# Sample heads: product order, stores by head, first keys turned under the norm; the first loads in turn; retention's gate and steps moved

## The reference

```
s     = einsum(q, k) * dmask                 # retention, within a chunk
inner = einsum(s, v)
kv    = einsum(k * d_in, v)                  # what the chunk adds to the state
state_new = g_chunk * state + kv             # an output of the program
cross = einsum(q * d_out, state)
on    = (o - mean(o)) / sqrt(var(o) + eps)   # by head, o = inner + cross
mix_r = silu(g) * on * gain                  # concatenated with attention's heads
p = softmax(q . [cache_k, k_new] + window)   # attention of the sample
mix_a = p @ [cache_v, v_new]
```

## Time and profile before

| what | value |
|---|---|
| median of 3 runs | 1917.29 us (1916.12 to 1919.46) |
| profiled execution | 1917.52 us, of which the span of the trace is 1915.7 us |
| busy over the span | PE 89%, PEld 72%, DVE 43%, ACT 29%, POOL 29% |
| granted PE clock, mean | 0.937 |
| bytes moved | 192.19 MB in 137588 packets, 100 GB/s over the span |

### The profile page before, as it was taken

The page is one execution under the profiler, slowest core; times in us unless marked ns, Lnnn a source line. Parts: engine busy times, 40 slices in busy tenths (PEclk is TensorE's granted clock), DMA queues, the critical chain, the costliest instruction groups (busy, mean ns, idle before and its releaser), DMA issues. The chain is left out here.

```text
span 1915.7 us, 22177 instructions
## 1 busy us (share of the span) xinstructions
PE 1698.6 (89%) x8272; PEld 1373.3 (72%) x8272; DVE 832.1 (43%) x1552; ACT 562.3 (29%) x828; POOL 554.9 (29%) x265
## 2 busy tenths in 40 slices
PE   6999999979898688876699689999999999999983
PEld 3778888857676566655588568787878788878862
DVE  4632212046465345566556223333333333333489
ACT  4322222225555155542344221111111111111121
POOL 0233333343000035585000232222222222222354
PEclk9999999979899589986799899999999999999997
DMA  8554433451100667763142211111111111111132
GB/s 290 203 178 155 171 124 121 160 142 56 56 0 24 177 201 219 221 205 111 65 149 80 67 44 44 44 44 44 44 44 44 44 44 44 44 44 44 44 88 93
DMA packets 137588, 192.19 MB, mean 100 GB/s; under 512 B 10034, under 2 KB 86882, under 8 KB 137387
## 3 DMA queue, kind: packets, MB, share of 16 engines
q1 hardware_dynamic: 125396, 168.83, 27.9%
q10 hardware_dynamic: 12128, 22.55, 3.2%
HBM read 162.42 MB, written 28.93 MB: 100 GB/s over the span
## 5 line engine op out<-in xcount | busy, mean ns | idle before, releaser
L2420 POOL TENSOR_TENSOR mlp_w_lo<-w_room,mlp_w_hi 128x2048 fp32r<-128x2048 f32 x31 | 143.7, 4637 | 320.6 <-ACT mlp_w_hi L2416 320.5
L2721 PE MATMUL ps<-mix_hi,mlp_w_hi 128*128 128x512 f32 x512 | 206.4, 403 | 15.1 <-DVE mlp_w_lo L2420 9.6
L2619 DVE TENSOR_TENSOR x<-x,ps 128x512 f32<-128x512 f32 x224 | 154.1, 688 | 141.9 <-PE ps L2792 141.2
L2598 DVE TENSOR_TENSOR mlp_h_lo<-mlp_pos,mlp_h_hi 128x512 fp32r<-128x512 f32 x64 | 69.3, 1083 | 332.8 <-ACT mlp_h_hi L2522 330.7
L2721 PE MATMUL ps<-mix_hi,mlp_w_lo 128*128 128x512 f32 x512 | 203.2, 397 | 0.0
L2721 PE MATMUL ps<-mix_lo,mlp_w_hi 128*128 128x512 f32 x512 | 202.8, 396 | 0.0
L584 POOL TENSOR_TENSOR inp_a_lo<-inp_room,inp_a_hi 128x2048 fp32r<-128x2048 f32 x24 | 111.6, 4649 | 273.8 <-ACT inp_a_hi L718 273.8
L2792 PE MATMUL ps<-mlp_w_hi,mlp_h_hi 128*128 128x512 f32 x448 | 175.8, 392 | 5.5 <-PE ps L2727 5.1
L2792 PE MATMUL ps<-mlp_w_hi,mlp_h_lo 128*128 128x512 f32 x448 | 174.5, 389 | 0.0
L2792 PE MATMUL ps<-mlp_w_lo,mlp_h_hi 128*128 128x512 f32 x448 | 174.3, 389 | 0.0
L637 PE MATMUL ps<-inp_whi,z_hi 128*128 128x512 f32 x384 | 150.3, 391 | 2.4 <-PE ps L637 1.3
(11 more groups left out here) (375 smaller groups left out, 3512.8 us busy)
## 6 DMA issues: line engine op xcount, KB each, us to landing
w_room<-in_w_ff SPq DMA_DIRECT2D x32, 1024.0 KB, 7.0
inp_room<-in_w_ada SPq DMA_DIRECT2D x16, 1024.0 KB
proj<-inp_row ACTq DMA_DIRECT2D x54, 256.0 KB, 2.5
x<-in_cache_k SPq DMA_DIRECT2D x48, 256.0 KB, 5.0
cache_V<-in_cache_v SPq DMA_DIRECT2D x48, 256.0 KB, 4.8
x<-in_x_prompt SPq DMA_DIRECT2D x16, 512.0 KB, 9.5
inp_room<-in_w_ada_f SPq DMA_DIRECT2D x8, 1024.0 KB
x<-in_w_in ACTq DMA_DIRECT2D x16, 512.0 KB, 6.7
```

The lines of the kernel that those rows point to most:

```text
L2420: pool.tensor_tensor(lo, raw, hi.bitcast(F32), ALU.subtract).then_inc(ready, 1)
L2598: dve.tensor_tensor(h_lo[s][:, j, cols], pos[u % 2][:], h_hi[s][:, j, cols].bitcast(F32), ALU.subtract).then_inc(h_ready, 1)
L2619: dve.tensor_tensor(dst, dst, ps[:, 5 + o % 3, :], ALU.add).then_inc(added, 1)
L2721: mm = pe.matmul(ps[:, u, :], w[:, k, j * P:(j + 1) * P], z[:, k, rows], start=(k == 0 and a == 0), stop=(k == KT - 1 and a == 2))
```

## The change

No product, no element-wise operation and no transferred byte of the computation is added or taken away; places, order and waits change.

In the sample heads: the products that are added to the states come before the scores; DVE takes the retention's queries ahead of the attention's, and the gate ahead of the masked scores; the outputs of heads 0, 1 and of heads 2, 3 lie in different banks, so that DVE takes moments and renews states of one pair while PE makes the other; each head's state is stored by itself, and only the next stage waits for these stores; the old states are loaded during the prompt's attention into a part of `x` that it has left; the keys of sequence 0 are loaded before anything is waited for. PE then turns the first three pieces of these keys into banks that are free (`EARLY_ROOMS`), ACT and DVE split them, around the norm; SP loads the first chunk of sequence 1. To make place, the keys lie at `KEYS_AT`, and bias, probabilities and states where the keys were.

In the sample attention: pair 0 starts at its fourth piece; the two tiles for the queries are zeroed by POOL and DVE at once; the bias is waited for where it is used; pair 0's loads of keys and values alternate.

In the retention: POOL waits for both `decayed_keys` before it multiplies the gate; ACT's root is a step of its own; the moments of head 3 come before the gates of heads 2 and 3.

```diff
+KEYS_AT = 3 * S
@@ stage_prompt_attention, SP
+                if pair == 3:
+                    sp.wait_ge(heads_free, 3)
+                    sp.wait_ge(kv_put[0], 64)
+                    smp.load_state(sp, io)
@@ stage_prompt_retention
-        mv = st.sb("mv", [P, TT, 6])
+        moment = [st.sb(f"mv{h}", [P, TT, 6]) for h in range(2)]
...
                 pool.wait_ge(sigmoid_done, a + 1)
+                pool.wait_ge(kd_done, 2)
                 pool.tensor_tensor(g[a][:], g[a][:], eg[a], ALU.mult).then_inc(gate_done, 1)
...
-            for n in range(RH):
-                normalise(n)
-                high_part(n)
+            square_root(0)
+            normalise(0)
+            high_part(0)
+            square_root(1)
+            normalise(1)
+            high_part(1)
+            square_root(2)
+            normalise(2)
+            square_root(3)
+            high_part(2)
+            normalise(3)
+            high_part(3)
...
             moments(2)
+            moments(3)
             gate(2)
-            moments(3)
+            gate(3)
             low_part(2)
-            gate(3)
             low_part(3)
@@ stage_sample_heads, SP
-            for b in range(2):
-                for q in range(4):
-                    sp.dma_start(state[RD * b:RD * (b + 1), q], st_in[b, :, q]).then_inc(s_in, 16)
+            for c in range(3):
+                load_cached(sp, io, "cache_k", K, k_in, 0, c)
             sp.wait_ge(smp.ready, 1)
...
-            for c in range(3):
-                load_cached(sp, io, "cache_k", K, k_in, 0, c)
-            sp.wait_ge(state_done, 1)
-            for b in range(2):
-                for q in range(4):
-                    sp.dma_start(st_out[b, :, q], state[RD * b:RD * (b + 1), q]).then_inc(put, 16)
-            sp.wait_ge(put, 16 * 10)
+            for h in range(RH):
+                sp.wait_ge(state_done, h + 1)
+                for b in range(2):
+                    sp.dma_start(st_out[b, :, :, h], state[RD * b:RD * (b + 1), :, h, :]).then_inc(state_put, 16)
+            sp.wait_ge(keys_turned, 2)
+            load_cached(sp, io, "cache_k", K, k_in, 1, 0)
+            sp.wait_ge(put, 32)
@@ stage_sample_heads, DVE
+            for pair in range(2):
+                heads = (2 * pair, 2 * pair + 1)
+                dve.wait_ge(o_made, pair + 1)
+                for h in heads:
+                    steps.done(dve.bn_stats(stats[:, h, :], o_room(h)))
+                dve.wait_ge(kv_made, 1)
+                for h in heads:
+                    dve.scalar_tensor_tensor(out=state[:, :, h, :], in0=state[:, :, h, :], scalar=GCHUNK_S[h],
+                                             in1=ps[:, 4:8, h * RV:(h + 1) * RV], op0=ALU.mult,
+                                             op1=ALU.add).then_inc(state_done, 1)
...
+            for k in range(EARLY):
+                dve.wait_ge(keys_hi, k + 1)
+                dve.tensor_tensor(keys_part(kT_lo, k), keys_room(k).rearrange("p (c x) -> p c x", c=4),
+                                  keys_part(kT_hi, k).bitcast(F32), ALU.subtract)
@@ stage_sample_heads, PE
+            for k in range(EARLY):
+                pe.wait_ge(k_in[k // 2], CHUNK_IN[k // 2])
+                if k == 1:
+                    pe.wait_ge(state_done, RH)
+                for c in range(4):
+                    for u in range(2):
+                        at = 2 * c + u
+                        mm = pe.transpose(keys_room(k)[:, at * P:(at + 1) * P], K[:, 2 * k + u, c * P:(c + 1) * P], ident[:])
+                mm.then_inc(keys_turned, 1)
@@ stage_sample_attention, SP
-            sp.dma_start(bias, io["bias_s"]).then_inc(tables, 16)
-            for c in range(3):
-                values(0, c)
+            values(0, 0)
+            keys(1, 1)
+            sp.wait_ge(state_put, 16 * 2 * RH)
+            sp.dma_start(bias, io["bias_s"]).then_inc(tables, 16)
+            keys(1, 2)
+            values(0, 1)
+            keys(2, 0)
+            values(0, 2)
+            keys(2, 1)
+            keys(2, 2)
+            values(1, 0)
@@ stage_sample_attention, POOL and DVE
+            pool.memset(q_lo[:].bitcast(F32), 0.0).then_inc(zeroed, 1)
...
-            for x in (q_hi, q_lo):
-                dve.memset(x[:].bitcast(F32), 0.0).then_inc(zeroed, 1)
+            dve.sem_inc(freed, EARLY)
+            dve.memset(q_hi[:].bitcast(F32), 0.0).then_inc(zeroed, 1)
             dve.wait_ge(zeroed, 2)
-            dve.wait_ge(tables, 16)
```

More of the change, by code:

```diff
@@ L1069, in group_norm @@
     e = steps.eng
-    for j in range(n):
-        steps.done(e.bn_stats(stats[rows, j, :], src(j)))
     steps.wait()
@@ L1109, in __init__ @@
             ("dout", [2, P]), ("din", [RH]), ("gch", [2]), ("gain", [RH])))
[L1110 removed]
+        first = 0
         self.v = arena[:, first:first + TT * 2 * RV].rearrange("p (t c) -> p t c", t=TT)
@@ L1487, in load, with load_state @@
             sp.dma_start(dst, io[n]).then_inc(self.tables, 16)
+    def load_state(self, sp, io):
+        src = io["state_ret"][0].rearrange("(q b) h d e -> b d q h e", b=2)
+        for b in range(2):
+            for q in range(4):
+                sp.dma_start(self.state[RD * b:RD * (b + 1), q], src[b, :, q]).then_inc(self.state_in, 16)
     def load_low(self, sp, io):
@@ L1575, in _ @@
             steps = Steps(dve, dve_s)
-            dve.wait_ge(smp.ready, 1)
-            dve.wait_ge(att_turned, 1)
-            for h in range(H):
-                rows = slice(HD * (h % 2), HD * (h % 2 + 1))
-                src = ps[rows, 0, (h // 2) * NS:(h // 2 + 1) * NS].rearrange("p (b t) -> p b t", b=DB)
-                steps.done(dve.tensor_scalar(q_blocks[rows, :, h // 2, h * DS:(h + 1) * DS], src, SCALE, None, ALU.mult))
-            steps.done(dve.tensor_copy(kT_new[:], ps[:, 0, 4 * NS:8 * NS].rearrange("p (c n) -> p c n", n=NS)))
             dve.wait_ge(ret_turned, 1)
@@ L1590, in _ @@
             signal(steps, qT_done)
+            dve.wait_ge(smp.ready, 1)
+            dve.wait_ge(att_turned, 1)
+            for h in range(H):
+                rows = slice(HD * (h % 2), HD * (h % 2 + 1))
+                src = ps[rows, 0, (h // 2) * NS:(h // 2 + 1) * NS].rearrange("p (b t) -> p b t", b=DB)
+                steps.done(dve.tensor_scalar(q_blocks[rows, :, h // 2, h * DS:(h + 1) * DS], src, SCALE, None, ALU.mult))
+            steps.done(dve.tensor_copy(kT_new[:], ps[:, 0, 4 * NS:8 * NS].rearrange("p (c n) -> p c n", n=NS)))
+            signal(steps, att_taken)
+            dve.wait_ge(sigmoid_done, 1)
+            steps.then(dve.tensor_tensor(eg[:], eg[:], x[:, GC:], ALU.mult))
+            steps.then(dve.tensor_tensor(eg[:], eg[:], gain[:], ALU.mult))
             dve.wait_ge(sT_made, 1)
@@ L1630, in _ @@
             mm.then_inc(ret_turned, 1)
-            pe.wait_ge(qT_done, 1)
-            pe.wait_ge(s_in, 128)
             vcols = lambda h: x[:, VC + h * RV:VC + (h + 1) * RV]
-            for h in range(RH):
-                mm = pe.matmul(ps[0:NS, 2, h * NS:(h + 1) * NS], kT[0:RD, h, :], qT[0:RD, h, :], start=True, stop=True)
-            mm.then_inc(sT_made, 1)
             for h in range(RH):
@@ L1640, in _ @@
             mm.then_inc(kv_made, 1)
+            pe.wait_ge(qT_done, 1)
+            for h in range(RH):
+                mm = pe.matmul(ps[0:NS, 2, h * NS:(h + 1) * NS], kT[0:RD, h, :], qT[0:RD, h, :], start=True, stop=True)
+            mm.then_inc(sT_made, 1)
+            pe.wait_ge(s_in, 128)
+            pe.wait_ge(att_taken, 1)
             pe.wait_ge(sT_done, 1)
             for h in range(RH):
-                out = ps[0:NS, 3, h * RV:(h + 1) * RV]
-                pe.matmul(out, sT[:, h * NS:(h + 1) * NS], vcols(h), start=True, stop=False)
+                pe.matmul(o_room(h), sT[:, h * NS:(h + 1) * NS], vcols(h), start=True, stop=False)
                 for b in range(4):
-                    mm = pe.matmul(out, q_masked[:, h, b, :], state[:, b, h, :], start=False, stop=(b == 3))
-            mm.then_inc(o_made, 1)
+                    mm = pe.matmul(o_room(h), q_masked[:, h, b, :], state[:, b, h, :], start=False, stop=(b == 3))
+                if h % 2:
+                    mm.then_inc(o_made, 1)
+            for k in range(EARLY):
+                pe.wait_ge(k_in[k // 2], CHUNK_IN[k // 2])
[6 more added lines that the diff above has]
+                mm.then_inc(keys_turned, 1)
             pe.wait_ge(on_ready, 1)
             for h in range(RH):
-                mm = pe.transpose(ps[:, 2, h * NS:(h + 1) * NS], on[:, h * RV:(h + 1) * RV], ident[0:NS, 0:NS])
+                mm = pe.transpose(ps[:, 0, h * NS:(h + 1) * NS], on[:, h * RV:(h + 1) * RV], ident[0:NS, 0:NS])
             mm.then_inc(o_turned, 1)
@@ L2008, in softmax_top @@
                     dve.wait_ge(turned, AT["P", j - 1, 1] + 1)
+                else:
+                    dve.wait_ge(tables, 16)
                 dve.memset(waited[:], 0.0)
@@ L2055, in _ @@
                 queries(i)
-                keys(i, 0)
-                keys(i, 1)
```

(5 more changed lines are left out.)

112 lines of the change are left out of this document (58 added, 54 removed).

## The result

The changed kernel takes **1892.38 us** (median of 4 runs, 1887.44 to 1895.26), the kernel before 1916.7 us beside it: a ratio of 0.987 (95% interval 0.985 to 0.988), 24 us less. The profiled execution took 1894.17 us, its span 1892.4, at a mean clock of 0.945. The forecast was 1893.4 us.

The account below looks back on a forecast made before the run. PE is near full from 1100 us on, so only its standstills between 617 and 950 us counted. 1917.5 less 11.5 (pair 0, sample heads included) less 12.6 (retention) gave 1893.4 us; range 1886 to 1901 us.

Parts of the forecast that it names:

- Part 1: Sample heads: outputs start 7.5 us earlier, after DVE's masked scores instead of loaded states; the stage gains 7.0 us.
- Part 2: Pair 0 of the sample attention: first scores 2.6 us after the start; ends 11.5 us earlier, sample heads' gain included.
- 6.9 us of products at half speed lose 3.4: Pair 0: clock stays low for 9.5 us after the stage's start, until 659, costing 3.4 us of the lead.
- The lead is carried through: Sample attention from pair 1 on: lists are as before, so the lead gained by pair 0 is kept.
- Part 3: Retention: shorter decayed_keys, then outputs and chunk products at full clock, gain 12.6 us; bounds 7.0 and 13.6.
- Steps at the end: End of retention: head 3's moments before gate 2 gain nothing else and cost 0.1 us; bounds -1 and +1.5.
- A: Sample heads: the clock rises, outputs take half of 9.9 us, 5.0 less; 1888.4 us, chance 0.10.
- B: Retention: PE restarts cold, so only the 7.0 us of decayed_keys is gained; 1899.1 us, chance 0.08.
- C: Retention: the wait moves with POOL to masked_scores(0, 0), leaving a gain of 2.6 us; 1903.4 us, chance 0.05.
- D: Pair 0: loads at 189 GB/s come 4.3 us after PE wants them; 1897.7 us, chance 0.05.
- E: Sample attention: the whole stage loads at 189 GB/s, 33 us more in four pairs; 1926 us, chance 0.02.
- F: Whole kernel: no effect, leads lost before the stages end by an unseen wait; 1917 us, chance 0.03.

Follow-up runs that it names:

- e6: The changed kernel with the old states loaded in the sample heads again, behind the tables; product order kept: 1890.64 us, ratio 0.987.
- e2: The changed kernel without POOL's wait for both decayed_keys in retention, all else kept: 1902.1 us, ratio 0.9922.
- e11: The changed kernel with ACT's sigmoid of the second gate half made twice, lengthening PE's gap in retention: 1894.5 us, ratio 0.9898.
- e9: The changed kernel with pair 0's loads in the old order, sequence 1's first keys no longer loaded in the heads: 1897.17 us, ratio 0.9898.
- e3: The changed kernel with ACT's copies of head pair 1's turned queries and keys ahead of the second gate half's sigmoid: 1888.35 us, ratio 0.9851.
- e4: The changed kernel with ACT's normalise(3) ahead of high_part(2) at the end of retention: 1887.26 us, ratio 0.9842.
- e1: The kernel before with only POOL's wait for both decayed_keys in retention added: 1905.69 us, ratio 0.995.

## Why the prediction was right, point by point

- **Part 1, -7.0: right, and for the reason given.** Between the marks -7.05. The outputs began 11.5 us after the heads' start instead of 18.4, behind DVE's masked scores and not behind the states. One reading was generous: the early load of states, told as if it belonged to the gain, has no share in it (e6).
- **Part 2, -11.5: right in mechanism, too small.** The marks give -13.7. The first scores came at 2.47 us, forecast 2.6. The term that was mis-sized is "6.9 us of products at half speed lose 3.4": I took the 9.5 us of low clock behind the stage's start as a fixed time, but in most executions the clock was low for 3.2 to 3.6 us of scores, which loses 1.6 to 1.8; with the 1.1 of the vanished wait that makes the +0.5 of the table. In e2 and e11 it was 5.9, and these are the two at 29.2. No wait for cached keys was left, and e9 shows that this hangs on the new loads.
- **"The lead is carried through": right.** Pairs 1 to 3 take 175 to 178 us in either kernel. The first profile seemed to lose 1.8 us there; with eight executions that is scatter.
- **Part 3, -12.6: two values, and the forecast near one.** With the clock full it is -13.5: 7.1 to 7.5 from the gap, 4.5 from the outputs, 1.7 from chunk products that took 3.33 us, not 3.96. In two of the eight executions with POOL's wait and the sigmoid ahead of the copies it is -9.0. The step that failed there is "PE starts the outputs of head 0 about 1.6 us after its last transpose": it follows DVE alone, and what ended last was ACT, with the sigmoid and, ahead of it, the gate's DMA. That holds for all eight. DVE's path by itself leaves 0.59 (e3), since `decayed_keys` takes 0.88 for both and not 2 x 0.96; that six executions had 1.1 to 1.5, near the forecast, is luck. The argument that a gap of that size keeps the clock is borne out up to 1.52 us and not at 2.13: in the first profile one of the signs of being wrong, a clock of 0.5 in these outputs, stood for 5.8 of their 8.5 us.
- **Steps at the end, +0.1: right**, with the reason given (ACT's order), and e4 shows what the reason was worth.
- **Rivals.** A is false: the heads' outputs ran at 0.50 to 0.53 with PE 6.00 of 6.00 us busy, and the clock rose only within the last of them (its eight products took 1.59 us, those of each head before 1.97), so the turns of keys behind had it full. The Trainium skill, TensorE: Matmul & The Clock Gate (The HAM clock gate), holds that sustained activity releases the low clock. By that rule A was likely; here PE had worked for some 20 us, with one wait of 1.75, before it rose. B came half true in two executions of eight. C is false: `masked_scores` takes 2.60 us for both with POOL at work (865.58) and 2.60 without (e2); only `decayed_queries(1)` waited, 2.78 against 1.23 in e2, where POOL was through. The Trainium skill, SBUF — State Buffer (Who interferes with whom), says that a DVE instruction with one SBUF input, outside the two-port modes, does not contend with GpSimd's, and that one with two does; the trace agrees, as the first takes its other input from PSUM. D and E are false: 276 and 269 GB/s in the first scores' windows, and no wait. By the figures shown D's loads would have come 4.7 us late (671 + 9.6 - 675.9), not 4.3; nothing hangs on it. F is false: the leads are there at the output projection.
- The sum was closer than its terms, by luck. In the profiled execution: -2.2 of scatter ahead of the heads, -14.25 from the heads' start to pair 0's mark (-11.5 forecast), +1.8 of scatter in pairs 1 to 3, -9.0 in retention (-12.6 forecast), -23.7 in all against -24.1: two misses that cancel. Over the repeats it is -13.7 and, where the clock stayed, -13.5: 27.2, to 1890.

## What to carry to other kernels

A wait that costs the clock is worth more than its length: 7 us off PE's wait brought 13.5 us of retention, and in two executions with 1 us more of it 4.5 of them were gone; so look at which engine ends last after the stall is gone, and take that away too. Moving a step on one engine brings nothing while the next engine's list still has the old order (e1 and e4); read both lists together. Where two executions of the same code differ by some us in a stage that the edit leaves alone, cut the trace at marks and use every run's profile as a repeat.

## What the runs showed of the hardware

Two DVE multiplications by a scalar from SBUF took 8.89 us beside POOL's two multiplications of the gate, and 0.88 where POOL waited for them; one semaphore wait makes and unmakes this (e1, e2). The clock fell in the middle of work: after the gap of 2.13 us the first 2.7 us of outputs ran at 0.98 and the next 5.8 at 0.50, with PE busy all the time; after 3.46 us and more it was low from the start. And the two executions that ran retention's first chunk products at full clock reached the wait sooner, waited longer, and took 4.5 us more for the stage than the five at 68.2; that the early full clock is the reason is read from the traces and tested by no run.
